# The first network's attention: the second tile's part moved between the first tile's expert picks, and one unit routed later

## What is computed

```
kv = rms_norm(x, norm_kv) @ w_kv                 # keys (normed, partly rotated) and values
proj = h @ w_in                                  # queries and a gate
s_own = where(kpos <= qpos, q @ k.T * scale, NEG)
x = x + (softmax(s_own) @ v * silu(gate)) @ w_out
```

```
q = xt @ w_q;  s1, s2 = q_a @ keys1.T, q_b @ keys2.T          # 8 heads
t1, i1 = top_k(s1, 16);  t2, i2 = top_k(s2, 16)
ts, sel = top_k(t1[:, None] + t2[None, :], 16);  idx = pairs of i1, i2 that sel names
act = gelu(u[idx] @ xt);  out = sum over heads, k of softmax(ts) * act * v[idx]
```

## Time and profile before

| what | value |
|---|---|
| median of 3 runs (range) | 1422.48 us (1420.62 to 1422.99) |
| the profiled execution | 1427.83 us, span 1426.0 |
| first pick issued / last landed | 641.2 / 1414.7 us |
| PE, DVE, ACT, POOL busy | 83%, 62%, 36%, 20% of the span |
| moved by DMA | 414.93 MB |

### The profile page before, as it was taken

The page is one execution under the profiler, slowest core; times in us unless marked ns, Lnnn a source line. Parts: engine busy times, 40 slices in busy tenths (PEclk is TensorE's granted clock), DMA queues, the critical chain, the costliest instruction groups (busy, mean ns, idle before and its releaser), DMA issues.

```text
span 1426.0 us, 23109 instructions
## 1 busy us (share of the span) xinstructions
PE 1188.5 (83%) x8702; PEld 795.0 (56%) x8702; DVE 886.7 (62%) x2284; ACT 508.4 (36%) x1526; POOL 287.5 (20%) x269
## 2 busy tenths in 40 slices
PE   7999998999999999999897878986666665656564
PEld 4445798987479988998675544754122222222111
DVE  7526766556563563147585487566777787777654
ACT  1214222211262143122442476324344444344334
POOL 0000000000000000001231334322354344443440
PEclk9899999999999999999998989998678778787867
DMA  8344100243324586779999999999999999999995
GB/s 314 129 150 148 47 3 3 76 158 122 119 89 131 196 301 214 238 266 399 365 421 413 394 393 379 421 420 423 413 425 425 423 426 424 424 425 426 425 425 245
DMA packets 82960, 414.93 MB, mean 291 GB/s; under 512 B 10847, under 2 KB 15327, under 8 KB 49761
## 3 DMA queue, kind: packets, MB, share of 16 engines
q0 software_dynamic: 37152, 269.50, 45.6%
q1 hardware_dynamic: 45554, 143.69, 28.4%
q10 hardware_dynamic: 144, 0.26, 0.0%
HBM read 412.36 MB, written 1.06 MB: 290 GB/s over the span
## 4 chain that ended last, share of the span: by engine, by line
PE 46%; DMA 30%; DVE 6%; issue 3%; ACT 3%; POOL 2%; POOLq 0%; DVEq 0%; ACTq 0%
DMA row<-peer_in,arena 14%; PE bank L1893 12%; DMA arena<-peer_in,arena 12%; PE bank L2915 7%; DMA ring<-stream_in 4%; PE bank L1425 3%; PE bank L1505 2%; PE bank L2803 2%; PE bank L1482 2%; PE bank L846 2%; PE bank L2081 2%; PE bank L655 1%; PE bank L645 1%; POOL arena L3235 1%; DVE arena L3193 1%
## 5 line engine op out<-in xcount | busy, mean ns | idle before, releaser
L2915 PE MATMUL bank<-arena 128*64 128x512 f32 x808 | 321.6, 765 | 153.1 <-ACT arena L3050 153.1
L3193 DVE CUSTOM_DVE_ANT_0 arena<-arena 128x1024 f32<-128x1024 f32 x202 | 246.6, 1224 | 153.7 <-DMA arena<-peer_in,arena 150.8
L3235 POOL DMA_INDIRECT arena<-peer_in,arena x202 | 219.7, 1088 | 561.3 <-PE bank L2915 371.2
L2915 PEld LDWEIGHTS bank<-arena 128*64 128x64 f32 x808 | 76.5, 160 | 323.1 <-issue 319.7
L1893 PE MATMUL bank<-arena,ring 128*128 128x128 f32 (+1 forms) x1984 | 239.8, 281 | 13.3 <-DMA ring<-stream_in 11.7
L1893 PEld LDWEIGHTS bank<-arena,ring 128*128 128x128 f32 x1984 | 232.2, 194 | 27.6 <-issue 14.5
L3034 ACT ACTIVATE arena<-arena 128x2 f32<-128x2 f32 (+1 forms) x130 | 26.4, 203 | 393.6 <-DVE arena L3193 393.5
L3038 ACT ACTIVATE arena<-arena 128x1 f32<-128x1 f32 x256 | 85.4, 380 | 4.3
L3043 ACT ACTIVATE arena<-arena 128x1 f32<-128x1 f32 x256 | 84.1, 375 | 6.8 <-DVE arena L3199 6.4
L2803 PEld LDWEIGHTS bank<-arena,ring 128*128 128x128 f32 x512 | 65.8, 209 | 34.6 <-issue 29.3
L2915 PE MATMUL bank<-row,arena 128*64 128x512 f32 x112 | 71.5, 774 | 7.1 <-ACT arena L3050 7.1
(11 more groups left out here) (395 smaller groups left out, 1856.6 us busy)
## 6 DMA issues: line engine op xcount, KB each, us to landing
ring<-stream_in SPq DMA_DIRECT2D x243, 512.0 KB, 4.7
ring<-stream_in SPq DMA_DIRECT2D x16, 384.0 KB, 5.6
arena<-peer_in,arena POOLq DMA_INDIRECT x202, 19.9
row<-rows_in SPq DMA_DIRECT2D x4, 512.0 KB, 18.2
ring<-stream_in SPq DMA_DIRECT2D x16, 128.0 KB, 7.4
cst<-cst_in SPq DMA_DIRECT2D x1, 1900.0 KB, 17.0
row<-rows_in POOLq DMA_DIRECT2D x2, 512.0 KB, 6.0
cst<-rg_w_in SPq DMA_DIRECT2D x1, 1024.0 KB, 6.7
```

The source lines that it names most:

```text
L2915: return nc.tensor.matmul(core.banks[2 * t + b][rows_of(j), :], diag[i % ND], places[seat[i]][:, D + b * 512:D + (b + 1) * 512], start=Fal ...
L3193: ins = nc.vector.tensor_tensor_reduce(out=row, in0=row, in1=X2[t][i % 2], scale=STEEP, scalar=0.0, op0=ALU.mult, op1=ALU.add, accum_out=d ...
L3235: pool.indirect_dma_start(out=places[seat[i]], out_offset=None, in_=g.names["peer"], in_offset=bass.IndirectOffsetOnAxis(ap=index[:, i:i + ...
```

## The change

**The first attention does tile 0 alone.** The values of tile 1, second half, are left out of the loop and made after the output projection of tile 0, with four slots read again (`rest_of_values`). Keys, queries and gate of tile 1 and the values of tile 0 are written to memory by four DMAs of POOL, 512 KB each (`spill`), and fetched by four more in front of pick 0 (`bring`), because their room is used by the second network's first pass; keys of tile 0 and values of tile 1 stay where they are. The first pass of ACT and DVE and POOL's key copies (L2665) wait for the four writes.

**Tile 1's attention is a generator `late_pass` on PE, ACT and DVE**, laid between the picks ahead of `second_pass`: one head per pick, the transposes 6 heads behind the scores and the products 9 to 10, then the output projection with its 8 slots read again, then the norm. RATE goes from 1.2 to 2.0.

**The gates' weights** (1 MB in `cst`) were kept for the second pass. Their room is now a seventh place for picks 0 to 31; then SP, waiting for the last use, loads them again, and from pick 46 on the room is a place again (before: from 16). Picks 32 to 45 have six places. Five more places open at pick 110 instead of 112.

**Distances in the second pass.** Gates and recurrence come ahead of the low projections. In its attention the transposes stand 6 steps behind the scores (5 before) and the product is one step later; DVE's masks follow at the pick of the scores' lag and the divisions 1 step behind them (2 before), ACT's part of the divisions 3 steps (4 before). The eight mixing matmul groups end in two banks instead of eight.

**Routing.** Unit 8, the second tile's first, was scored around pick 82 and routed in unit 6. Now it is scored around pick 104 and routed in unit 7, ahead of unit 9: DVE takes 10 pieces of a route in the second and third pair of unit 7, and 6 in its last four.

The core of the diff (the first `late_pass` is PE's, the second DVE's):

```diff
+        def value_rows(t, half, kp, slot):
         for half in range(2):
+            ts = range(TT - half)
...
+        rest_of_values((0, 1))
+        pe.wait_ge(g.summed_c.handle, 1)
+        nc.tensor.matmul(bank[:, 0:NM + P], cst("ones"), g.squares_c[:, 0, :], start=True, stop=True).then_inc(*full(("ss_c", 0)))
+        rest_of_values((2, 3))
...
+        def late_pass():
+            pe.wait_ge(brought.handle, 64)
+            copied(pe, ("vb", 1, 1))
+            for i in range(H + 9):
+                if i < H:
+                    late_scores(i)
+                if 6 <= i < H + 6:
+                    late_turn(i - 6)
+                if i >= 10 and i % 2 == 0:
+                    late_weigh((i - 10) // 2)
+                g.at["late", i] = g.now
+                yield ("late", i), 1
+            yield ("late", H + 8), 4
+            for m in range(KT):
+                late_out(m)
+                yield 1.0
...
+        def late_pass():
+            for i in range(H + 9):
+                yield ("late", i), 1
+                if i < H:
+                    mask(i, 1)
+                if 1 <= i < H + 1:
+                    divide(i - 1, 1)
+                if i == 16:
+                    late_gated(0)
...
+        kept = [(rotated["kb"][:, 1, :, :], rotated_up, 4), (rotated["qb"][:, 1, :, :], rotated_up, 8)]
+            pool.dma_start(tiles(g.spill[n], P), src).then_inc(*spilled.dma())
+    def bring(pool):
+        pool.wait_ge(spilled.handle, 64)
+        pool.wait_ge(g.rnn_ready[0].handle, 1)
+        pool.dma_start(late(0, D), g.spill[0]).then_inc(*brought.dma())
...
-    START, RATE = -7, 1.2
+    START, RATE = -7, 2.0
-    GATED, LATER = 16, 112
+    DROPPED, GATED, LATER = 32, 46, 110
...
-                if n + 3 < N and n + 3 != HP:
+                if n == HP - 1 and q < 2:
+                    query(HP + 1, q)
+                if n == HP - 1 and q == 2:
+                    scores(HP + 1)
+                if n + 3 < N and n + 3 not in (HP, HP + 1):
...
+            if n == HP - 1:
+                routing = itertools.chain(route(HP), [None], routing)
+                    steps = (0, 10, 10, 0, 6, 6, 6, 6)[q]
...
+        core.load_weights(sp, g.stream, core.slot_no["again", ("gr", 0)])
+        sp.wait_ge(used.handle, gates_wait)
+        g.load_gates(sp)
```

637 lines of the change are left out of this document (384 added, 253 removed).

## The result

The changed kernel takes 1433.11 us, median of 4 runs (1431.92 to 1435.05); the kernel before takes 1422.07, median of 4 (1420.62 to 1422.99). The ratio is 1.0080, 95% interval 1.0062 to 1.0097. It is slower, by 11 us; 1414.5 was forecast, and the range ended at 1428. The profiled execution took 1431.92 us, its span is 1430.1.

The account below looks back on a forecast made before the run. PE was taken to bound the kernel up to the first pick, DMA from there on. -25.8 + 12.3 + 5.7 = -7.8 us, taken from the 1422.5 median, gave 1414.7, said as 1414.5; range 1405 to 1428.

Parts of the forecast that it names:

- First part, -25.8: Up to the first pick: work leaving PE makes this part 25.8 us shorter, bounds 18 and 27.3; first pick about 615.4.
- The step from the span to the median: Whole execution: the three runs' median, 1422.5, lies 5.3 us lower than the profiled execution, so 1420.0 became 1414.7.
- Spilling, 0: Before the first pick: writing tensors to memory and fetching them back costs 0, bounds 0 and 4.9 us.
- Bytes, +12.3: Behind the first pick: 5.24 MB of weights read again cost 12.3 us at 425 GB/s.
- The second unit's late routing, 0: Picks 112 to 127: unit 8's route shares them with unit 9's, DVE 41 us of DMA's 44; costs 0.
- Does DMA stay full: +5.7, bounds -5 and +20: First tile's picks: DMA loses 5.7 us more beside the moved work; called the largest unknown.
- the 395 that were named as a sign: Over the first tile: DMA under 395 GB/s would show the prediction wrong.
- DVE without a gap there: Sign for the 20 us after the seventh pick: DMA is idle while DVE works without a gap.
- The attention of the second network keeps its rate of a head per pick: Second network's attention: keeps most of the 7.8 us lost in 788 to 880; longer distances -1, bounds 0 and -4.
- The second pass starts at pick 30 ... DMA stays the bound, by 8%: Rest of the first tile: four weight slots per pair, DMA 9.9 us against PE 9.1 per pair.
- Six places, 1 us: Picks 32 to 45: six buffers instead of seven, with weights beside them, cost 1 us.
- rival B: First tile becomes bound by DVE and ACT; decides from 13.5 us of added loss, with 19: 1428; 20%.

Follow-up runs that it names:

- e1: Changed kernel with DVE's division two picks after its mask instead of one, in both attentions; ratio 1.0021 to the kernel before.
- e6: e1 with DVE's convolution of the second tile two picks earlier in DVE's order; ratio 0.9964 to the kernel before, 1415.8 us.
- e11: e6 with seven eighths of the first output projection's second weight reading left out; ratio 0.9948 to the kernel before.
- e9: Kernel before with DVE's division one pick after its mask instead of two, in the second network's attention; ratio 1.0031 to the unedited kernel before.
- e2: Changed kernel with PE's second-tile gate matmuls held back nine picks and the gates' place used from pick 48 instead of 46; ratio 1.0097 to the kernel before.
- e10: e6 with six places instead of seven for picks 0 to 31 and no second reading of the gates' weights; ratio 1.0017 to the kernel before.
- e7: e1 with 2 instead of 8 steps of the second unit's routing on DVE before its first dot; ratio 1.0031 to the kernel before.

## Why the prediction was wrong

- **First part, -25.8.** Right in mechanism and nearly in size: 27.7 us, just past the bound of 27.3. Two errors in it met by luck. The loop with its projection gave 10.6 us and not 11.9: a turn lost 1.29 us instead of 1.49, because the smaller matmuls do not shrink by their share (the product takes 0.37 us where 0.27 was counted, the scores 0.42 for 0.33). The end of the stage made up for it: the last stretch of 4.47 us is 1.78 now, where 1.1 was to be gained and 1.5 lost for the last heads' cover. The first pick came at 603.8 and not at 615.4: 1.9 us by this, 0.5 in the next stage, and 9.2 because the profile of before had a lower clock in its first 200 us, which I did not see. The step from the span to the median took 5.3 us off for the whole execution and did not say where they were.
- **Spilling, 0.** Right: POOL issues the last two reads at 572.50 and 573.02, they land in 7.7 us (median of the four), and 430.07 to 603.83 takes 173.76 us, where 467 to 641 took 174.
- **Bytes, +12.3.** Right as bytes: 5.24 MB more behind the first pick. As time it could not be shown by itself.
- **The second unit's late routing, 0.** Right: picks 104 to 127 move 420 to 426 GB/s. POOL does wait 5.46 us for the routing at pick 128, which the prediction had as a sign of being wrong, but DMA stayed full over it.
- **Does DMA stay full: +5.7, bounds -5 and +20.** This step failed: +29.9. DMA moved 379 GB/s over the first tile, under the 395 that were named as a sign. I counted what DVE has to do in the first unit and took its steps to run without a wait ("DVE without a gap there"; it is busy 15.4 of the 20 us from 610). With the division two picks after its mask the first unit lost 4.7 to 5.9 us more than before (e1, e6, e11), and 5.7 were forecast. With the wait it lost 11.5.
- **"The attention of the second network keeps its rate of a head per pick ... its longer distances are taken at -1, bounds 0 and -4."** This is the sentence that failed most. I took each distance to have grown. The one between DVE's mask and DVE's division had shrunk from two picks to one, as the section on the change says itself, and ACT's exponentials lie between. e1 and e9 show what it costs from both sides: 8.4 us of the 11.4 in both attentions, and 4.4 us by this number alone in the kernel before. With the division moved back the second network's attention loses what it lost before: 9.8 us in columns 48-87 (e1), against 9.3.
- **"The second pass starts at pick 30 ... DMA stays the bound, by 8%."** Right for its long runs (picks 48 to 63 move 404 GB/s), wrong at one place: the order of its stages had changed too, with the gates directly behind the input stage, and PE's wait for the convolution cost 5 of the 8.5 us (e6, by the traces).
- **Six places, 1 us.** No run measured it for picks 32 to 45. e2, with six places up to pick 47, lost 4.6 us in picks 32 to 47, and the kernel before, with seven and other work, 4.3. The same price per pick would be far too low in the first unit, where e10 puts the seventh place at 6.5 to 10 us.
- **The rivals.** B came nearest by its number (1428). Its cause, DVE and ACT too busy, is not that of the 8.4 us: ACT is busy 0.67 of 64-87, DVE 0.70, and with the same work and other distances the stretch loses half. For what is left in the first unit load is likely but not shown: DVE is busy 46.4 of 51.2 us there in e1, and e7 only moved the loss inside it.
- What stays open: of the 30 us of added loss e6 still has 15.8, more than the 13.5 from which rival B was to decide, and no experiment names one cause for them. 4.9 lie in the first unit, 9.4 in picks 32 to 87. By kind of work the attention now loses 11.8 us (48-87) where it lost 9.3, so most of the rest is picks 32 to 47 with their 8.3 us, where the second pass now begins; before, it began beside pick 0. PE's 2.57 us for ACT there were seen and not tried.

The Trainium skill (SBUF — State Buffer, "SBUF: two separate sides") has DVE's operations on two ports hold up POOL's descriptors. The issues in the first unit take up to 1.90 us, but so they did before (1.98). POOL is busy 17.16 us with 17 issues there, 1.2 more than at 0.94 each, and it waited 38.2 us for PE, so such a rule does not explain the loss of 18.4. The same page's 358 GB/s of memory to one core ("A bandwidth-pool intuition that's wrong (but worth ruling out)") is again not what is measured: 425 GB/s over 260 us in the first table of windows.

## What to carry to other kernels

Where several in-order engines share steps with a pacing loop, count the distance of every pair of producer and consumer, on each engine, and through the engine between them; one distance that fell by a pick cost 8.4 us here, in 32 heads, while others were made longer. A step that waits costs what stands behind it in its order, so look first at which pick's work stands behind it. A count of busy time is a lower bound: for the first unit it was right to 1 us once the waits were out, and 6 us short with them. Compare stretches by kind of work as well as by place; a column that grew may hold what another gave up.
